# A hybrid attention and convolution layer: in each attention step the products with the values come ahead of the turn of q and k

## The reference

```python
h = rms_norm(x, attn_norm_g)
q, k, v, a, g = split(h @ w_in)                 # 3 x 512 and 2 x 512 columns
q, k = rms_norm(q per head), rms_norm(k per head)
attn = combine(band(q, k, v, w, r) for w, r in ((128, 1), (512, 4), (2048, 16)))
u = a * sigmoid(g)
c = silu(layer_norm(causal_depthwise(u, 31 taps)))
x = x + concat(attn, c) @ w_out
h = rms_norm(x, ffn_norm_g)
x = x + (silu(h @ w_gate) * (h @ w_up)) @ w_down
```

## Time and profile before

| | |
|---|---|
| median of 3 runs | 1425.53 us (1424.42 to 1427.17) |
| the profiled execution | 1423.0 us |
| its span, first to last instruction | 1420.9 us |
| TensorE busy | 1317.1 us (93%) |
| VectorE, ScalarE, POOL busy | 667.1, 314.3, 474.0 us |
| granted TensorE clock, mean | 0.974 of full speed |

### The profile page before, as it was taken

One profiled execution on the slowest core, in us unless ns is written; L12 is line 12 of the kernel. 1 busy time (PEld: TensorE's weight loads), 2 busy tenths in 40 slices (PEclk: granted clock), 3 DMA queues, 4 the chain that ended last, 5 costly groups with the idle time before them and its releaser, 6 DMA issues.

```text
span 1420.9 us, 22561 instructions
## 1 busy us (share of the span) xinstructions
PE 1317.1 (93%) x9084; PEld 1253.3 (88%) x9084; DVE 667.1 (47%) x1227; ACT 314.3 (22%) x715; POOL 474.0 (33%) x307
## 2 busy tenths in 40 slices
PE   6999789799795869999999999999999999999998
PEld 6999667677674559999999999999999999999998
DVE  6697867767678445583141414131313131313234
ACT  6212434444344325342101010101000000000000
POOL 0232522424215322533624242424242424333220
PEclk9999999999897879999999999999999999999999
DMA  7214143332435201038511410141114111411103
GB/s 223 64 53 145 31 150 101 111 104 77 138 104 213 83 18 43 31 119 282 194 44 60 149 60 31 52 157 46 45 45 163 44 47 35 171 33 60 38 0 126
DMA packets 50693, 131.07 MB, mean 92 GB/s; under 512 B 14480, under 2 KB 26640, under 8 KB 50064
## 3 DMA queue, kind: packets, MB, share of 16 engines
q1 hardware_dynamic: 45088, 95.47, 20.1%
q10 hardware_dynamic: 5504, 34.11, 7.1%
HBM read 120.09 MB, written 43.28 MB: 115 GB/s over the span
## 4 chain that ended last, share of the span: by engine, by line
PE 82%; DVE 10%; issue 2%; ACT 2%; POOL 2%; DMA 1%; SPq 0%; ACTq 0%; DVEq 0%; POOLq 0%
PE ps L330 25%; PE ps L332 25%; PE ps L331 25%; DVE uc L1249 5%; PE ps L743 1%; PE ps L808 1%; PE ps L739 1%; PE ps L815 1%; DVE ml_c L1494 1%; POOL zst L537 1%; PE ps L849 1%; PE ps L753 1%; DMA out_nk_p<-zst 1%; DVE tb L1337 1%; PE ps L718 1%
## 5 line engine op out<-in xcount | busy, mean ns | idle before, releaser
L637 POOL TENSOR_TENSOR wf<-raw,small 128x1024 fp32r<-128x1024 f32 x60 | 113.9, 1898 | 433.2 <-PE ps L332 423.4
L1573 DVE TENSOR_TENSOR pr<-ps,sg 128x362 f32<-128x362 f32 (+1 forms) x66 | 35.4, 536 | 411.0 <-ACT sg L1209 411.0
L330 PE MATMUL ps<-mh_a,wf 128*128 128x362 f32 (+1 forms) x624 | 207.7, 333 | 14.0 <-DVEq L1442 3.7
L1249 DVE SCALAR_TENSOR_TENSOR uc<-uc,small 128x1024 f32<-128x1024 f32 x240 | 215.1, 958 | 0.1
L332 PE MATMUL ps<-mh_a,wf 128*128 128x362 f32 (+1 forms) x624 | 205.5, 329 | 0.0
L331 PE MATMUL ps<-ml_a,wf 128*128 128x362 f32 (+1 forms) x624 | 205.4, 329 | 0.0
L331 PE MATMUL ps<-ml_c,wf 128*128 128x362 f32 (+1 forms) x624 | 203.9, 327 | 0.0
L332 PE MATMUL ps<-mh_c,wf 128*128 128x362 f32 (+1 forms) x624 | 203.9, 327 | 0.0
L330 PE MATMUL ps<-mh_c,wf 128*128 128x362 f32 (+1 forms) x624 | 203.5, 326 | 0.0
L1591 DVE TENSOR_TENSOR y<-ps,y 128x362 f32<-128x362 f32 (+1 forms) x264 | 139.4, 534 | 107.9 <-PE ps L332 107.9
L332 PE MATMUL ps<-ah,wf 128*128 128x364 f32 (+1 forms) x528 | 174.0, 330 | 0.0
(11 more groups left out here) (150 smaller groups left out, 2118.7 us busy)
## 6 DMA issues: line engine op xcount, KB each, us to landing
raw<-in_w_stream SPq DMA_DIRECT2D x94, 512.0 KB, 3.5
skt<-in_kT_c SPq DMA_DIRECT2D x32, 384.0 KB, 5.3
sv<-in_v_c SPq DMA_DIRECT2D x32, 384.0 KB, 6.8
xr<-in_xT SPq DMA_DIRECT2D x8, 544.0 KB, 4.3
out_yT<-y SPq DMA_DIRECT2D x8, 544.0 KB, 2.7
y<-in_xT SPq DMA_DIRECT2D x1, 3264.0 KB, 15.3
out_nv_p<-vn SPq DMA_DIRECT2D x32, 64.0 KB, 1.8
out_nk_p<-zst SPq DMA_DIRECT2D x32, 64.0 KB, 1.6
```

The source lines that it names most:

```text
L330: e.matmul(out, wh, mh_, start=first, stop=False)
L637: pool.tensor_tensor(hi(m), src, zeros, ALU.add).then_inc(w_hi, 1)
L1249: dve.scalar_tensor_tensor(out=dst, in0=src, scalar=w, in1=dst, op0=ALU.mult, op1=ALU.add).then_inc(s, 1)
L1573: dve.tensor_tensor(pr[:, k6 % 2, 0:bn], bank(2 * (k6 % 2) + 1, bn), sg[:, k6 % 2, 0:bn], ALU.mult).then_inc(gu_pr, 1)
```

## The change

In TensorE's loop, `values(n - 1)` now stands ahead of `turn`:

```diff
                 turn_probs(n)
                 if s in (1, 6):
                     turn_sample(p, s // 5)
-                if turn_at(p, s) is not None:
-                    turn(turn_at(p, s))
                 if fills:
                     fill(s, 1)
                 if n >= 1 and s not in (1, 6):
                     values(n - 1)
+                if turn_at(p, s) is not None:
+                    turn(turn_at(p, s))
                 if fills:
                     fill(s, 2)
```

## The result

The changed kernel takes 1413.41 us in the median of 4 runs (1412.49 to 1414.81); before had 1425.11 in the same comparison. The medians are 11.7 us apart. The ratio is 0.9916, 95% interval 0.9899 to 0.9934: faster by 12.0 us (9.4 to 14.4). The profiled execution took 1412.49 us, 10.5 less than that of before, with a span of 1410.4.

The account below looks back on a forecast made before the run. TensorE, busy 93% of the span, was taken as the bound. Filled gaps of 10.2 us less 1.8 at boundaries gave 8.4 off the profiled 1423.0, so 1414.6; against the median 1417.1, range 1414.5 to 1421.5.

Parts of the forecast that it names:

- Steps 2 to 8: Pairs 0 to 2: values fill TensorE's gap ahead of the turn; 3.39 us gained a pair, 10.2 for three.
- The overlap of 0.07 us: Successive TensorE instructions overlap by 0.07 us, so a filled gap of 0.62 us is worth 0.69.
- The slack of 0.3 us ahead of `qkv`: Tightest step: scores still cover ScalarE's two copies of q and k with about 0.3 us left; costed at nothing.
- Step 9 into step 0: Boundary between pairs: late turn delays weight cuts and POOL's subtractions; VectorE through 0.6 us later, three times, 1.8 us lost.
- the four taps 9.9 us: Step 0 on VectorE: four taps alternating with POOL's subtractions would end 9.9 us after they began, not 8.95.
- The old sum: Taps and subtractions of the boundary added up for the kernel before: 265.0 us, against 264.95 in the rows.
- the boundary costs nothing, or gains: Rival for step 9 into step 0: free first tap pays for the delay; 1414 to 1415.3 us, chance 0.15.
- The bridge from profile to median: Median of runs, 1425.5 us, lies 2.5 above the profiled execution's 1423.0; 1414.6 thus became 1417.1.
- The clock rival: TensorE's granted clock falls differently behind VectorE's stretches; 1418.7 to 1421.7 us, or the other way; chance 0.15.
- The rival "slower": Each boundary: a subtraction falls between VectorE's last tap and normalisation, +3.3 us three times; 1429.7 us, chance 0.05.
- The range's lower end: Lower bound of the forecast time's range: 1414.5 us.

Follow-up runs that it names:

- e5: Changed kernel with each turn moved behind the next step's scores, right ahead of the next `qkv`; 1426.13 us in one run.
- e1: Changed kernel with the old order (turn ahead of values) in steps 9 and 0 alone; 1414.43 us, ratio 0.9921.
- e3: Changed kernel with POOL's gain of k behind its third subtraction instead of ahead of it; 1411.12 us in one run.
- e11: Kernel before, unchanged, run once more for a second profile; 1426.78 us.
- e12: Kernel before, unchanged, run once more for a third profile; 1424.76 us.
- e2: Kernel before with the new order (values ahead of turn) in steps 9 and 0 alone; 1424.54 us, ratio 0.9993.
- e6: Changed kernel with the same 24 taps a pair spread otherwise, none in step 0; 1391.98 us, ratio 0.9761.
- e9: Changed kernel with the taps moved out of step 0 and the old order, turn first, in steps 9 and 0; 1389.94 us, ratio 0.9743.
- e8: Kernel before with the same 24 taps a pair spread otherwise, none in step 0; 1400.61 us, ratio 0.9819.

## Why the prediction was wrong

**Steps 2 to 8: right.** The sum was 3.39 us a pair. Without the clock's part the profiles show 3.27, 3.26 and 3.28, in all 9.8 for 10.2. The single gains: step 2 0.36, step 3 0.60, step 4 0.65, step 5 0.54, step 7 0.66, step 8 0.45. The overlap of 0.07 us was right; the turn takes 0.36 behind the values where it took 0.34 ahead of them. The slack of 0.3 us ahead of `qkv` held; e5 shows the price where it does not. e1 shows that this part is the whole gain.

**Step 9 into step 0: the step that failed.** "VectorE is through 0.6 us later than before, three times: 1.8 us lost." Measured: -0.12, -0.15 and +0.03 us, in sum 0.2 gained. All that was said about the turn, the copies, the cuts and the first subtraction came true within 0.1 us. The addition behind it was mis-sized: I gave the four taps 9.9 us. With the strict turns I assumed they take 9.25 (e3): the large tap between two subtractions takes 1.1 and not 1.35, and each subtraction ends 2.2 to 2.3 us behind what it waited for, where I had added 2.35 to 2.5. The old sum came out at 265.0 all the same by luck: in the kernel before the third tap takes 1.5 behind the second subtraction and the third subtraction 2.2 behind that tap, where I had put 1.35 and 2.37.

The order of the turns was not what I had either. In the changed kernel the small tap slips in ahead of the third subtraction, because POOL's gain of k had been held up, and the normalisation stands behind that subtraction. (The expectation of e1 has the first normalisation slip in too; the 2.43 us of its row in the changed kernel show that it did not.) Either way VectorE's next mask pass starts 9.76 to 9.78 us after its first tap, where my sum had it at 10.5 (9.9 and the 0.6 of a free normalisation): 0.7 us too much, three times. In the kernel before it starts 9.46 after, so the stretch is 0.3 us longer, and it begins 0.47 us earlier: 0.17 gained, near the 0.12 and 0.15 measured. The rival "the boundary costs nothing, or gains" was what happened, and had 0.15; the time still lies below its 1414 to 1415.3.

**The bridge from profile to median: the second miss.** The sum was made against a profiled execution 2.5 us below the median, and I carried that distance over unchanged. e11 and e12 show that part of it came from one place in pair 3, where the kernel before usually loses 3.2 us and did not in the first profile, and where the changed kernel loses 1.4. So the typical gain at this place is some 1.8 us larger than the one against the first profile. Three profiles with the old order in steps 2 to 8 lose 3.2 to 3.3 there (e2, e11, e12) and one nothing; four with the new order lose 1.4 to 1.6 and one, e3, gains. It is not the order alone: with the taps moved, e6 has the new order and loses 3.0, e9 has it too and loses 1.3, and e8 with the old one loses 3.3. How much of it is the change and how much the luck of 0.15 us, and why the clock falls in the one case and not in the other, stays open.

**The clock rival** was priced against the change, though it allowed for the other way: by the count above 0.8 us less was lost, not more. **The rival "slower"** did not occur; a subtraction did come between VectorE's taps and its normalisation, as it had it, but in place of a wait of the taps, not on top.

Together: 8.4 forecast; +2.0 for the boundaries, -0.4 for the steps, +0.8 for the clock, and between the first profile's pair 3 (-1.4), the start (-0.3) and the part behind attention (+1.3) a remainder near 0 gives the 10.5 of the profiles. The last of these need not come from the change: from step 8's scores of pair 3 to the end the kernel before took 898.4, 901.2 and 897.2 us in its three profiles, the changed one 897.1. The range's lower end allowed for a free boundary or for some scatter, not for both.

## What to carry to other kernels

Where two users of a PSUM bank follow one another with an eviction between them, put independent work of the eviction's length between them, and no more: too early costs the wait, too late costs the next user's. Where two engines block each other, write out both rows of instructions in turns to the end of the stretch, with the work that follows it, before charging a delay to it; the delay of one entry often only changes who waits. And look at more than one profile of before where the sum is to be right to 0.1%: one race in it may go either way.

## What the runs showed that was not expected

- A start 0.15 us earlier or later decides between 2.8 and 4.93 us for the same two instructions of VectorE beside POOL's subtractions, and with the clock behind it 3.2 us of an execution.
- Of 1,024-column and 64-column taps, both wait for a subtraction of POOL's: the small one, 0.27 us alone, took 2.39.
- The clock's loss within a pair's step 2 differs between pairs and executions of one kernel (5.24 to 6.75 us for the same `qkv`), yet its sum, counted as above, lies between about 6.5 and 8.0 us in nine profiles of kernels with the taps in place. The exception is e5, where three `qkv` of step 7 alone cost 8. With the taps moved (e6, e8, e9), TensorE's longest wait between 176 and 400 us falls from 6.2 to under 1.8 us, and the granted clock there is 0.98, 1.00 and 0.99, where the kernel before and the changed one have 0.95. It does not stay at full speed throughout: in e9 it is 0.50 from 337.5 to 340.9 us.
